# One gather per chosen expert for both expert tables, in eight shared buffers

## The chip, the core and the metric

The kernel runs on one core of a Trainium2 chip. The metric is the device time of one execution, in microseconds; lower is better. A core has five engines that each run their own list of instructions in order (TensorE, VectorE, ScalarE, GpSimd and SyncE; in the profile PE, DVE, ACT, POOL and SP) and sixteen DMA engines that move data between memory and the core's SBUF. The engines meet only through semaphores.

## The reference

One step of a two-layer trunk on 640 tokens (512 latent and 128 context tokens), all in float32. Each layer mixes tokens and then applies PEER, a lookup into 16384 experts. The change touches PEER alone:

```python
q = (xb @ wq).reshape(PEER_BLOCK, PEER_HEADS, 2, PEER_HALF)
s = jnp.einsum('thpd,hpnd->thpn', q, keys)
s_top, i_top = lax.top_k(s, PEER_TOPK)
cand = s_top[:, :, 0, :, None] + s_top[:, :, 1, None, :]
best, pos = lax.top_k(cand.reshape(..., PEER_TOPK * PEER_TOPK), PEER_TOPK)
g = jax.nn.softmax(best, axis=-1)
ue = jnp.take(u_tab, idx, axis=0)
ve = jnp.take(v_tab, idx, axis=0)
act = gelu(jnp.einsum('td,thkd->thk', xb, ue))
return jnp.einsum('thk,thkd->td', g * act, ve)
```

For each of 640 tokens and 8 heads, 16 experts are chosen. Each chosen expert has a row of 1024 numbers (4 KB) in table u, whose dot product with the token gives a weight, and a row of 1024 in table v, which is summed with that weight.

## The kernel before

The function `experts` does PEER for one layer; it runs twice. Its work is cut into 40 units: 8 heads (h) by 5 blocks of 128 tokens (b), a token on each partition. In a unit there are 16 choices s. For one unit n the steps are these.

- PE computes queries (`ask`, one call for two blocks, so three calls in five units, 48 matmuls each) and scores (`score`), three units ahead (LEAD).
- DVE turns scores into 16 row numbers per token (`choose(n + 2)`, some 25 short instructions that each wait for the one before), two units ahead. The row numbers are in `ex_index`.
- POOL issues indirect DMAs (`gather`): for each s one from `peer_u` into a slot of `u_row` and one from `peer_v` into a slot of `v_row`, each of 128 rows of 4 KB (0.5 MB). There are 8 slots for u (in `ring`) and 8 for v (in `early`). The v gathers run one unit behind the u gathers: POOL's list takes two u gathers of unit n and two v gathers of unit n - 1 in turn. A u slot is free when its dot product is made (`u_used`), a v slot when its matmuls are made (`v_used`).
- DVE makes 16 dot products, one per u slot, then waits for ACT's gelu on all 16, multiplies by the softmax share, and signals the 16 weights (`w_ready`). Then it runs `choose(n + 2)` and `gather_sum(n - 1)`, which adds the finished PSUM of a unit to the output.
- ACT makes one diagonal matrix for each choice (the identity times the column of weights), in 8 buffers.
- PE multiplies each diagonal with its v slot, and sums the 16 products of a unit in PSUM (`sums`, two matmul calls of 512 columns, four matmul records in the profile).

So DVE works on unit n while PE works on unit n - 1. The order on each engine is the order in which the code is written; nothing is scheduled otherwise. When the last unit's dots are done, PE still has its 16 choices to sum, and DVE uses this time for the layer norm of the earlier blocks (`residual`, `normal_rows`, `modulated`, `new_low_of`).

## Time and profile before

| | |
|---|---|
| Time, median of 3 runs | 6708.51 us (6702.12 to 6709.55) |
| The profiled execution, span | 7135.4 us |
| PE, DVE, ACT, POOL busy | 81%, 57%, 26%, 39% of the span |
| Gathers | 2560, 1342.34 MB |

The profiled execution is one execution with the profiler on. Its own time is its span, 7135.4 us, from the first instruction to the last; no other time of it is given. It is 427 us longer than the median of the unprofiled runs. Two stretches belong to `experts`: about 1648 to 3600 us and about 5182 to 7135 us.

The profile says for each engine how long it was busy, and for each instruction what ended the idle time before it. In a row of the timeline the number in square brackets is that idle time. A share of DMA near 1 means that all sixteen DMA engines had packets all the time. PEclk is TensorE's granted clock: 1.00 is 2.4 GHz and 0.50 is 1.2 GHz.

### The profile page before, as it was taken

The page shows a single profiled execution, that of the slowest core. Times are in us where ns is not written, and L with a number is a line of the kernel's source. Part 1 is how long each engine was busy: PE and PEld are TensorE (multiplying, and loading weights), DVE is VectorE, ACT ScalarE, POOL GpSimd, SP SyncE. Part 2 cuts the span into 40 slices and gives each one's busy share as a digit, 9 for nine tenths or more (in the row PEclk, how much of TensorE's full clock was granted, in tenths as well). Part 3 has the DMA queues.
Part 4 walks back from the last instruction along what each step waited for, and adds up shares of the span by engine and source line. Part 5 has one row for each costly group of instructions (what it writes and reads, how often), then busy time and mean ns, then how long its engine had stood idle before and what let it go on. Part 6 is the DMA issues. An engine that isn't in the chain of part 4 may idle for free. (4 is left out here: it accounts for less than half of the span.)

```text
span 7135.4 us, 94928 instructions
## 1 busy us (share of the span) xinstructions
PE 5756.5 (81%) x36912; PEld 4065.6 (57%) x36912; DVE 4044.6 (57%) x8218; ACT 1880.9 (26%) x3574; POOL 2797.2 (39%) x2909
## 2 busy tenths in 40 slices
PE   7889999795777777777788899997867777777776
PEld 7779999593333333333387799986833333333332
DVE  3654334557665666566636634346576566656666
ACT  1662112412222122212226621124121222122211
POOL 0330000014666666666613300000166666666665
PEclk8999999997998999999999999999988999999999
DMA  4002121327999999999921012222389999999998
GB/s 173 17 33 84 72 75 69 144 99 287 355 354 352 361 351 358 357 357 364 387 85 39 23 72 83 75 81 90 107 329 351 357 357 357 347 355 355 353 372 318
DMA packets 425299, 1632.88 MB, mean 229 GB/s; under 512 B 47648, under 2 KB 69600, under 8 KB 412260
## 3 DMA queue, kind: packets, MB, share of 16 engines
q0 software_dynamic: 368640, 1342.34, 49.4%
q1 hardware_dynamic: 56214, 284.46, 10.9%
q8 instruction: 297, 4.87, 0.3%
q14 instruction: 148, 1.21, 0.1%
HBM read 1611.68 MB, written 17.56 MB: 228 GB/s over the span
## 5 line engine op out<-in xcount | busy, mean ns | idle before, releaser
L1984 PE MATMUL ex_ps_y<-early,peer_small 128*128 128x512 f32 x5120 | 2534.4, 643 | 887.5 <-DMA early<-in_peer_v,ex_index 626.0
L1984 PEld LDWEIGHTS ex_ps_y<-early,peer_small 128*128 128x128 f32 x5120 | 993.4, 204 | 2348.5 <-issue 1416.5
L1834 DVE CUSTOM_DVE_ANT_0 ring<-ring,ex_ps_h 128x1024 f32<-128x1024 f32 x1280 | 1510.6, 1219 | 696.3 <-DMA ring<-in_peer_u,ex_index 545.1
L1637 POOL DMA_INDIRECT early<-in_peer_v,ex_index x1280 | 1234.7, 965 | 792.8 <-issue 355.8
L1637 POOL DMA_INDIRECT ring<-in_peer_u,ex_index x1280 | 1219.8, 953 | 706.5 <-issue 369.8
L1935 ACT ACTIVATE peer_small<-ident,ex_w 128x128 f32<-128x128 f32 x1280 | 441.2, 392 | 1477.2 <-PE ex_ps_y L1984 707.7
L1117 POOL TENSOR_SCALAR ring<-ring 128x2048 f32<-128x2048 f32 x2 | 10.8, 5387 | 1623.7 <-DMA ring<-mod_rows 1623.7
L258 PE MATMUL conv_ps<-h_high,conv_wh 128*128 128x320 f32 x1024 | 317.1, 310 | 9.3 <-DVE conv_wl L156 9.3
L258 PE MATMUL conv_ps<-h_low,conv_wh 128*128 128x320 f32 x1024 | 316.6, 309 | 0.0
L258 PE MATMUL conv_ps<-h_high,conv_wl 128*128 128x320 f32 x1024 | 316.5, 309 | 0.0
L1928 ACT ACTIVATE ex_act<-ex_dot 128x16 f32<-128x16 f32 x80 | 17.2, 216 | 1116.0 <-issue 944.7
L1965 PE MATMUL ex_ps_q<-h_high,ex_wh 128*128 128x256 f32 (+1 forms) x768 | 255.4, 333 | 57.7 <-DVE h_low L156 29.4
L258 PE MATMUL rf_ps<-rf_wh,h_high 128*128 128x256 f32 x960 | 268.2, 279 | 14.0 <-DVE rf_wl L156 14.0
L258 PE MATMUL rf_ps<-rf_wl,h_high 128*128 128x256 f32 x960 | 267.7, 279 | 0.0
L258 PE MATMUL rf_ps<-rf_wh,h_low 128*128 128x256 f32 x960 | 267.6, 279 | 0.0
L1965 PE MATMUL ex_ps_q<-h_low,ex_wh 128*128 128x256 f32 (+1 forms) x768 | 238.5, 311 | 26.5 <-issue 26.2
L1965 PE MATMUL ex_ps_q<-h_high,ex_wl 128*128 128x256 f32 (+1 forms) x768 | 239.7, 312 | 24.4 <-issue 24.1
L1038 POOL TENSOR_TENSOR room<-room,rec_bounds 128x256 f32<-128x256 f32 x80 | 64.7, 809 | 437.6 <-ACT room L1032 437.3
L1965 PEld LDWEIGHTS ex_ps_q<-h_high,ex_wh 128*128 128x128 f32 x768 | 171.0, 223 | 68.5 <-issue 37.9
L156 DVE TENSOR_TENSOR rf_wl<-ring,rf_wh 128x2048 fp32r<-128x2048 f32 (+1 forms) x36 | 74.7, 2085 | 238.5 <-ACT rf_wh L285 238.5
L156 DVE TENSOR_TENSOR conv_wl<-ring,conv_wh 128x2048 fp32r<-128x2048 f32 (+1 forms) x42 | 91.7, 2188 | 203.1 <-ACT conv_wh L285 203.1
L258 PEld LDWEIGHTS conv_ps<-h_high,conv_wh 128*128 128x128 f32 x1024 | 193.5, 189 | 9.8 <-DVE conv_wl L156 9.8
(335 smaller groups left out, 12091.3 us busy)
## 6 DMA issues: line engine op xcount, KB each, us to landing
ring<-in_w_in SPq DMA_DIRECT2D x54, 2048.0 KB, 7.8
ring<-in_mod_w SPq DMA_DIRECT2D x22, 2048.0 KB, 7.6
ring<-in_w_branch SPq DMA_DIRECT2D x12, 2048.0 KB, 7.8
ring<-in_peer_u,ex_index POOLq DMA_INDIRECT x1280
early<-in_peer_v,ex_index POOLq DMA_INDIRECT x1280
room<-in_peer_wq SPq DMA_DIRECT2D x14, 1024.0 KB
ring<-in_w_out SPq DMA_DIRECT2D x4, 2048.0 KB, 8.3
room<-mod_rows SPq DMA_DIRECT2D x12, 512.0 KB, 7.9
```

The costliest lines, as they stand in the source:

```text
L156: return nc.vector.tensor_tensor(low, full, high.bitcast(F32), ALU.subtract)
L258: last = nc.tensor.matmul(ps[:, at:at + cols], lhs, rhs, start=k == 0 and n == 0, stop=k == KT - 1 and n == 2)
L1038: step(nc.gpsimd.tensor_tensor(kk[:, m, at], kk[:, m, at], lb[:, 1, at], ALU.mult))
L1117: step(P_.tensor_scalar(vec[:, :, 1, :], vec[:, :, 1, :], 1.0, None, ALU.add))
L1637: nc.gpsimd.indirect_dma_start(rows[slot], None, table, bass.IndirectOffsetOnAxis(ap=index[n % 4][:, s:s + 1], axis=0)).then_inc(arrived[s ...
L1834: V.tensor_tensor_reduce(out=row, in0=row, in1=ps_h[:], scale=1.0, scalar=0.0, op0=ALU.mult, op1=ALU.add, accum_out=dot[n % 2][:, s:s + 1] ...
L1928: act.activation(act_v[n % 2][:], dot[n % 2][:], ACT.Gelu).then_inc(gelu_done, 1)
L1935: act.activation(diag[s % DIAGS], ident[:], ACT.Copy, scale=wgt[n % 2][:, s:s + 1]).then_inc(diag_ready, 1)
L1965: last = nc.tensor.matmul(ps_q[:, a, 0:width], w[h % 2][:, k, w_cols], h_split[x][:, k, toks], start=k == 0 and m == 0, stop=k == KT - 1 a ...
L1984: last = nc.tensor.matmul(ps_y[n % 2][:, c:c + 512], diag[s % DIAGS], v_row[s % V_SLOTS][:, c:c + 512], start=s == 0, stop=s == TOPK - 1)
```

## The change

The two tables are joined on the host into one, `peer_uv`, whose row is the u row and then the v row of an expert (8 KB). One gather fetches both into one of 8 slots; the slots lie in the same memory as the 16 of before. The slot is free when PE's matmuls on its v half are done. The v gathers are no longer a unit behind, so the dots and the sums of a unit run side by side: ACT makes gelu, weight and diagonal for each choice by itself, as soon as its dot is made. The softmax shares are made ahead (`soften`, `shares`). `ask` is split into two halves at s = 2 and s = 5, `score` is one choice later, and the work behind the last units' dots is arranged anew. `choose` is written in 16 parts, but all parts still run one after the other behind the unit's dots, with the same instructions.

```diff
-        U_SLOTS = V_SLOTS = DIAGS = 8
-        u_row, v_row = ([room[:]... for s in range(4)] for rooms in (ring, early))
+        SLOTS = DIAGS = 8
+        pair_row = [room[:]...[:, s * 2 * D:(s + 1) * 2 * D] for room in (*ring, *early) for s in range(2)]
+        u_row, v_row = ([row[:, side * D:(side + 1) * D] for row in pair_row] for side in range(2))
...
-                for n in range(units + 1):
-                    if n < units:
-                        pool.wait_ge(routed, n + 1)
-                    for s in range(0, TOPK, 2):
-                        if n < units:
-                            if TOPK * n + s >= U_SLOTS:
-                                pool.wait_ge(u_used, TOPK * n + s + 2 - U_SLOTS)
-                            for j in (s, s + 1):
-                                gather(u_row, u_in, T["peer_u"], n, j)
-                        if n:
-                            if TOPK * (n - 1) + s >= V_SLOTS:
-                                pool.wait_ge(v_used, TOPK * (n - 1) + s + 2 - V_SLOTS)
-                            for j in (s, s + 1):
-                                gather(v_row, v_in, T["peer_v"], n - 1, j)
+                for n in range(units):
+                    pool.wait_ge(routed, n + 1)
+                    for s in range(TOPK):
+                        if TOPK * n + s >= SLOTS:
+                            pool.wait_ge(v_used, TOPK * n + s + 1 - SLOTS)
+                        nc.gpsimd.indirect_dma_start(pair_row[s % SLOTS], None, T["peer_uv"], ...)
...
                         V.tensor_tensor_reduce(out=row, in0=row, in1=ps_h[:], ...
-                               op1=ALU.add, accum_out=dot[n % 2][:, s:s + 1]).then_inc(u_used, 1)
+                               op1=ALU.add, accum_out=dot[n % 2][:, s:s + 1]).then_inc(dotted, 1)
+                        if s == 7 and n + 1 < units:
+                            shares(n + 1)
                         behind_dot(n, s)
-                    dve.wait_ge(gelu_done, n + 1)
-                    V.reciprocal(total[n % 2][:], total[n % 2][:]).then_inc(recip_done, 1)
-                    V.scalar_tensor_tensor(wgt[n % 2][:], act_v[n % 2][:], total[n % 2][:], soft[n % 2][:], ...).then_inc(w_ready, 1)
-                    if n + 2 < units:
-                        choose(n + 2)
+                    for part in range(TOPK if n + 2 < units else 0):
+                        choose(n + 2, part)
...
-                    act.wait_ge(u_used, TOPK * (n + 1))
-                    act.activation(act_v[n % 2][:], dot[n % 2][:], ACT.Gelu).then_inc(gelu_done, 1)
-                    act.wait_ge(w_ready, n + 1)
                     for s in range(TOPK):
+                        act.wait_ge(dotted, r + 1)
+                        act.activation(act_v[n % 2][:, at], dot[n % 2][:, at], ACT.Gelu).then_inc(gelu_done, 1)
+                        act.wait_ge(gelu_done, r + 1)
+                        act.activation(wgt[n % 2][:, at], act_v[n % 2][:, at], ACT.Copy, scale=share[n % 2][:, at]).then_inc(weighed, 1)
+                        act.wait_ge(weighed, r + 1)
+                        act.activation(diag[s % DIAGS], ident[:], ACT.Copy, scale=wgt[n % 2][:, at]).then_inc(diag_ready, 1)
...
-                        if s == 2 and n and n + LEAD < units and where(n + LEAD)[1] % 2 == 0:
-                            ask(n + LEAD)
-                        if s == TOPK - 4 and n + LEAD < units:
+                        if s in (2, 5) and n and n + LEAD < units and where(n + LEAD)[1] % 2 == 0:
+                            ask(n + LEAD, (0,) if s == 2 else (1,))
+                        if s == TOPK - 3 and n + LEAD < units:
                             score(n + LEAD)
...
+        "peer_uv": np.concatenate([a["peer_u"], a["peer_v"]], axis=-1).reshape(DEPTH * EXPERTS, 2 * D),
```

What this does to the order is best seen on POOL and ACT. POOL, first layer, before: the end of unit 0's u gathers and the start of unit 1, where v gathers of unit 0 come in between (`ring_6` and `ring_7` hold u slots, `early_387` and `early_388` v slots, the number behind `ex_index` tells the unit).

```order
L1637 DMA ring_7<-in_peer_u,ex_index_394 128x1024 x4
L1637 DMA ring_6<-in_peer_u,ex_index_395 128x1024 x2
L1637 DMA early_387<-in_peer_v,ex_index_394 128x1024 x2
L1637 DMA ring_6<-in_peer_u,ex_index_395 128x1024 x2
L1637 DMA early_387<-in_peer_v,ex_index_394 128x1024 x2
L1637 DMA ring_7<-in_peer_u,ex_index_395 128x1024 x2
L1637 DMA early_388<-in_peer_v,ex_index_394 128x1024 x2
```

The same place in the changed kernel (the numbers behind the names are given anew in each build):

```order
L1643 DMA early_379<-in_peer_uv,ex_index_386 128x2048 x2
L1643 DMA early_380<-in_peer_uv,ex_index_386 128x2048 x2
L1643 DMA ring_6<-in_peer_uv,ex_index_387 128x2048 x2
L1643 DMA ring_7<-in_peer_uv,ex_index_387 128x2048 x2
L1643 DMA early_379<-in_peer_uv,ex_index_387 128x2048 x2
```

Half as many gathers, each twice as wide, and none of them a unit behind. ACT, one unit of the first layer before: the exponential, the gelu of all 16 choices, and 16 diagonals in a row.

```order
L1924 ACT_TABLE_LOAD
L1924 ACTIVATE ex_soft_406,ex_total_408<-ex_centred_400 128x16
L1928 ACT_TABLE_LOAD
L1928 ACTIVATE ex_act_404<-ex_dot_402 128x16
L1899 ACTIVATE ex_ps_h<-room_2 128x1024
L1935 ACTIVATE peer_small<-ident,ex_w_410 128x128 x7
```

The start of a unit in the changed kernel:

```order
L1944 ACT_TABLE_LOAD
L1944 ACTIVATE ex_soft_399,ex_total_401<-ex_centred_391 128x16
L1976 ACT_TABLE_LOAD
L1976 ACTIVATE ex_act_396<-ex_dot_394 128x1
L1980 ACTIVATE ex_w_404<-ex_act_396,ex_share_402 128x1
L1984 ACTIVATE peer_small<-ident,ex_w_404 128x128
L1976 ACTIVATE ex_act_396<-ex_dot_394 128x1
L1980 ACTIVATE ex_w_404<-ex_act_396,ex_share_402 128x1
L1984 ACTIVATE peer_small<-ident,ex_w_404 128x128
```

There are now three short instructions for each of the 16 choices, each behind the one before.

## Rows read from the trace of the kernel before

**Rows 1.** The page: span, busy time of each engine, gather queue (packets, MB, share).
```profile
span 7135.4 us, 94928 instructions
PE 5756.5 (81%) x36912; PEld 4065.6 (57%) x36912; DVE 4044.6 (57%) x8218; ACT 1880.9 (26%) x3574; POOL 2797.2 (39%) x2909
...
q0 software_dynamic: 368640, 1342.34, 49.4%
```
**Rows 2.** Stretches: length, busy time (count) of each engine, clock, DMA share, GB/s.
```profile
2500.00:3000.00 500.00, 381.02 (x1048) 182.79 (x1046) 318.07 (x767) 108.52 (x245) 320.06 (x335) 0.94 0.94 354
...
3500.00:3550.00 50.00, 35.20 (x69) 13.96 (x68) 36.64 (x51) 10.20 (x24) 31.51 (x31) 0.86 1.00 395
```
**Rows 3.** Gathers and matmuls by line, first layer: count, ns min/median/max, first to last start.
```profile
L1637 POOL DMA_INDIRECT ring<-in_peer_u,ex_index x640: 935/941/1992, 1648.0 to 3530.3; - x160
...
L1984 PE MATMUL ex_ps_y<-early,peer_small x2560: 589/592/1223, 1682.3 to 3578.9; 128*128 128x512 f32 x197
```
**Rows 4.** The same view, dot products, first layer.
```profile
L1834 DVE CUSTOM_DVE_ANT_0 ring<-ring,ex_ps_h x640: 1208/1218/1223, 1659.9 to 3543.6; 128x1024 f32<-128x1024 f32 x160
```
**Rows 5.** Timeline of POOL: start, us, engine, line, what, [idle before and what ended it].
```profile
2310.31 0.94 POOL L1637 DMA_INDIRECT ring<-in_peer_u,ex_index  x1 [0.30 <-issue]
2315.55 0.94 POOL L1637 DMA_INDIRECT early<-in_peer_v,ex_index  x1 [4.31 <-PE ex_ps_y L1984]
```
**Rows 6.** Timeline of PE: sums.
```profile
2313.31 3.70 PE L1984 MATMUL ex_ps_y<-early,peer_small 128*128 128x512 f32 x8 [1.40 <-DMA early<-in_peer_v,ex_index]
2319.75 4.12 PE L1984 MATMUL ex_ps_y<-early,peer_small 128*128 128x512 f32 x8 [2.74 <-DMA early<-in_peer_v,ex_index]
```
**Rows 7.** Stretches as in rows 2: PE nearly idle, right after it, and in full work.
```profile
2323.70:2327.20 3.50, 0.17 (x1) 0.00 (x0) 3.50 (x7) 0.40 (x1) 2.81 (x3) 1.00 0.98 382
2328.30:2331.60 3.30, 3.30 (x6) 1.24 (x5) 3.25 (x7) 0.40 (x1) 2.39 (x4) 0.50 1.02 401
2347.60:2351.30 3.70, 3.66 (x8) 1.44 (x8) 0.40 (x2) 2.03 (x5) 2.59 (x3) 1.00 1.02 409
```
**Rows 8.** Two calls of `ask` in the same view.
```profile
2355.90:2361.80 5.90, 5.90 (x51) 5.66 (x50) 4.84 (x26) 0.38 (x2) 4.57 (x5) 1.00 0.66 211
2261.40:2280.80 19.40, 7.89 (x51) 6.97 (x50) 13.80 (x24) 0.00 (x0) 11.87 (x13) 0.73 1.02 406
```
**Rows 9.** ACT groups, first layer: count | busy us, mean ns | idle before.
```profile
L1935 ACT ACTIVATE peer_small<-ident,ex_w 128x128 f32<-128x128 f32 x640 | 221.1, 393 | 752.0 <-PE ex_ps_y L1984 376.9 <-DMA scan_bmask<-in_bmask 222.4 <-issue 152.0
...
L1928 ACT ACTIVATE ex_act<-ex_dot 128x16 f32<-128x16 f32 x40 | 8.6, 216 | 558.1 <-issue 462.9 <-DVE ex_dot L1834 95.1
```
**Rows 10.** Timeline of DVE: one choice, its first instruction and what follows it.
```profile
2407.12 0.42 DVE L1674 COPY peer_small<-ex_ps_s 128x256 f32<-128x256 f32 x1 [8.28 <-remote]
...
2417.46 1.22 DVE L1742 TENSOR_TENSOR main<-main,ex_ps_y 128x1024 f32<-128x1024 f32 x1
```
**Rows 11.** DVE groups in the choices of the first layer, columns as in rows 9.
```profile
L1691 DVE MAX8 ex_best<-peer_small 128x8 f32<-128x256 f32 x40 | 17.1, 428 | 25.5 <-DVE peer_small L1688 16.0 <-remote 5.8 <-issue 1.0
L1696 DVE MAX8 ex_best<-peer_small 128x8 f32<-128x256 f32 x40 | 17.1, 428 | 10.7 <-remote 5.1
L1674 DVE COPY peer_small<-ex_ps_s 128x256 f32<-128x256 f32 x40 | 16.9, 423 | 153.8 <-remote 143.5 <-issue 7.9 <-PE ex_ps_s L1977 2.4
L1683 DVE MATCH_VALUE_LOAD ex_topi<-ex_top,peer_small 128x8 f32 x160 | 13.6, 85 | 21.1 <-issue 5.4 <-DVE ex_top L1679 5.3
L1687 DVE CAST ex_topf<-ex_topi 128x32 f32<-128x32 uint32 x40 | 7.6, 190 | 66.0 <-remote 55.9 <-issue 6.3 <-DVE ex_topi L1683 3.1
```
**Rows 12.** Timeline of DVE, end of the first layer.
```profile
3545.46 1.28 DVE L1774 SCALAR_TENSOR_TENSOR room<-room,norm_mv,room 128x1024 f32<-128x1024 f32 x1
...
3561.69 1.23 DVE L1781 TENSOR_TENSOR main<-main,ring 128x1024 f32<-128x1024 f32 x1
...
3579.82 1.21 DVE L1742 TENSOR_TENSOR main<-main,ex_ps_y 128x1024 f32<-128x1024 f32 x1
...
3599.34 1.22 DVE L156 TENSOR_TENSOR h_low<-ex_ps_h,h_high 128x1024 fp32r<-128x1024 f32 x1 [3.12 <-ACT h_high L1947]
```

More of the change, by code:

```diff
@@ L1547, in experts @@
         total = [sb(f"ex_total{j}", [P, 1]) for j in range(2)]
+        share = [sb(f"ex_share{j}", [P, TOPK]) for j in range(2)]
         wgt = [sb(f"ex_w{j}", [P, TOPK]) for j in range(2)]
@@ L1707, in choose @@
[L1707 to L1711 removed]
+                            last = V.max_index(top_i[:, a, 8:16], top[:, a, 8:16], lists[:, a, :])
@@ new lines, in choose @@
+                        chosen(4, last)
+                    if part == 5:
+                        behind(4)
+                        V.tensor_copy(top_f[:], top_i[:])
+                        chosen(5, V.tensor_tensor(cand[:].rearrange("p (i j) -> p i j", i=TOPK), top[:, 0, :].unsqueeze(2).to_broadcast([P, TOPK, TOPK]),
+                                                  top[:, 1, :].unsqueeze(1).to_broadcast([P, TOPK, TOPK]), ALU.add))
+                    if part == 6:
+                        behind(5)
+                        dve.sem_inc(picking, 1)
+                        chosen(6, V.max(best[:, 0:8], cand[:]))
@@ new lines, in choose @@
+                    if part == 13:
+                        behind(12)
+                        chosen(13, V.tensor_tensor(hit[:], hit[:], top_f[:].unsqueeze(2).to_broadcast(full), ALU.mult))
+                    if part == 14:
+                        behind(13)
+                        chosen(14, V.tensor_reduce(num[:], hit[:], AX.X, ALU.add))
+                    if part == 15:
+                        behind(14)
+                        chosen(15, V.scalar_tensor_tensor(num[:, 0], num[:, 0], float(P), num[:, 1], ALU.mult, ALU.add))
+                        behind(15)
+                        V.tensor_scalar(index[n % 4][:], num[:, 0], base[:, bass.ds(l, 1)], None, ALU.add).then_inc(routed, 1)
@@ L1823, in _ @@
                 dve.wait_ge(loaded, 48)
-                choose(0)
+                for part in range(TOPK):
+                    choose(0, part)
                 head_low_of(2)
                 head_low_of(3)
-                choose(1)
+                for part in range(TOPK):
+                    choose(1, part)
                 for n in range(units):
@@ L1854, in _ @@
                 normal_rows(2)
+                normal_rows(3)
                 if goes_on:
-                    dve.wait_ge(u_used, TOPK * units)
                     dve.wait_ge(vec_in, 64)
@@ L1860, in _ @@
                 onward(modulated, 1)
-                gather_sum(units - 2)
-                residual(3)
+                gather_sum(units - 1)
+                residual(4)
                 onward(new_low_of, 0)
                 onward(new_low_of, 1)
-                inverse(1, 3, 4)
-                normal_rows(3)
-                gather_sum(units - 1)
-                residual(4)
+                inverse(1, 4, 5)
+                normal_rows(4)
+                onward(modulated, 4)
                 onward(new_low_of, 2)
                 onward(new_low_of, 3)
-                inverse(2, 4, 5)
-                normal_rows(4)
-                onward(modulated, 4)
                 onward(new_low_of, 4)
@@ new lines, in _ @@
+                        act.wait_ge(weighed, r + 1)
+                        if r >= DIAGS:
+                            act.wait_ge(v_used, r + 1 - DIAGS)
+                        act.activation(diag[s % DIAGS], ident[:], ACT.Copy, scale=wgt[n % 2][:, at]).then_inc(diag_ready, 1)
+                        if s == 9 and n and n + LEAD < units and where(n + LEAD)[1] % 2 == 0:
+                            turn(n + LEAD)
+                        if s == 10 and b == 2 and h + 2 < PH:
+                            high(h + 2)
@@ L1942, in _ @@
+                        if s == 12 and n == units - 1:
+                            roots(4, 0, 4)
                 for b in range(NB):
                     if b == 2:
-                        roots(4, 3, 4)
+                        roots(5, 4, 5)
                     if goes_on:
@@ L1960, in ask @@
                         pe.wait_ge(turned, job)
-                    for a in range(2):
+                    for a in sides:
                         w_cols, toks = slice(a * P, (a + 1) * P), slice(b * P, b * P + width)
```

196 lines of the change are left out of this document (107 added, 89 removed).

## The prediction

> **What bounds the kernel now.** I read the page first, then the stretches, then the groups by line and last the timeline of single units. The page shows [rows 1] that no engine is full: PE 81% over the span, DVE 57%. The stretches show the reason: inside the expert work [rows 2] the DMA engines have packets 94% of the time over 500 us, at 354 GB/s, while PE is busy 76% and DVE 64%. So the gathers bound it, nearly. Their cost per unit comes out in two ways. The queue row [rows 1] gives the gathers 49.4% of sixteen engines' span, 0.494 x 7135.4 = 3525 us, over 80 units 44.1 us, over 16 choices 2.75 us for the 1 MB (u and v) of one choice. The full rate seen is 409 GB/s at share 1.02, in the last of [rows 7], which makes 1.049 MB / 409 = 2.56 us a choice and 41.0 us a unit. A layer's expert work, from the first gather at 1648.0 to the end of the last sum at 3579.5, takes 1931.5 us [rows 3], 48.3 us a unit. So some 4 us a unit are not transfer. They are bubbles such as the 4.31 us in which POOL waits for a v slot [rows 5], and single stalls of PE inside `ask` (19.4 us for work that takes 5.9 elsewhere [rows 8]).
>
> The profiled execution (its own time is its span) is 7135.4 us, 427 us over the median of 6708.5. The other stages move little data and their PE work is dense; I put all of the 427 us on the 80 units, 5.3 us each. An unprofiled unit of before is then 48.3 - 5.3 = 43.0 us, close to the 41.0 of pure transfer. That is an assumption, and much hangs on it: it leaves the old kernel only 2 us a unit to lose.
>
> **The change, part by part.** *Gathers.* The bytes stay the same. Half the packets and half the POOL instructions go (1280 x (0.94 + 0.30) = 1587 us of POOL time [rows 5]), but POOL was at 64% [rows 2] and no row shows the DMA waiting for it for long. What an 8 KB packet costs is not in the trace. From above: as much per byte as now, 2.75 us a choice; from below: the best rate of [rows 7], 2.56. I take 2.56 unprofiled, because the unprofiled unit of 43.0 leaves no room for 2.75 (16 x 2.75 = 44.0). What one `DMA_INDIRECT` of 8 KB rows costs POOL lies between 0.94 us (same number of rows) and twice that; I take 0.94.
>
> *Slots.* This is the part that decides. Before, u slots were free after a dot, and v slots filled behind them, so DMA had work while DVE chose. Now all 8 slots wait for one chain: dot, ACT, PE. While DVE runs the choice and `gather_sum`, no dot is made, and so no slot comes free; DMA has at most 8 choices of work, 8 x 2.56 = 20.5 us. I follow one unit from its first dot, with 8 slots full:
> - first dot 1.22 us [rows 4]; gelu 0.22, weight 0.22 (taken as the gelu), diagonal 0.39 [rows 9] and three hand-overs of some 0.1, together 1.1; the matmuls of a choice 1.85 us at full clock (8 records, two choices, in 3.70 [rows 6]). PE has been idle since the last sums, though: in [rows 7] a stretch with 0.17 us of PE work at clock 1.00 is followed by one at 0.50, that is 1.2 GHz. So 3.5 us for the first. Slot 0 is free after 5.8 us.
> - POOL issues; a gather into an idle queue was issued at 2315.55 [rows 5] and its matmul began at 2319.75 [rows 6], 4.2 us. 8 KB rows add half of 2.56: 5.5 us. Choice 8 is there at 11.3 us.
> - choices 9 to 15 follow at 2.56 each: 17.9 us, plus 0.6 as the second slot is freed at low clock too.
> - last dot 1.22, then the choice, then `gather_sum` 1.15 before the next dot.
> That makes 32.2 us plus the choice. The choice has the same 25 instructions. The undisturbed one takes 10.3 us, from 2407.12 to 2417.46 [rows 10]. Stalls inside it are in [rows 11]: 25.5 + 10.7 + 21.1 + 66.0 = 123 us over 40 units, 3.1 us each, of which about 0.7 is the ordinary hand-over: 2.4 us of stall, 12.7 us on average. Since the 5.3 us that the unprofiled unit lacks must come off something, I believe most of these stalls to belong to the profiled execution, and take 10.8. The unit is 43.0 us.
>
> *Queries.* `ask` costs 5.9 us when undisturbed [rows 8], in three of five units, and now stands in the chain that frees slots. Split in halves of some 2.9 us it delays the next slots by about what DMA can cover with the two slots already freed (5.1 us). From below nothing, from above the whole stall of [rows 8] in some units; I take 0.4 us a unit on average. Unit: 43.4 us.
>
> *Things that go.* The wait of DVE for the 16 gelus and the wait of the choice for its scores (153.8 us a layer before L1674 [rows 11]) go; both lay beside DMA that was working, so they pay nothing by themselves. The new gelus are 16 a unit, on an ACT at 22% [rows 2]: hidden, as 1.1 us a choice is less than PE's 1.85. The exponential with its two table loads comes while DVE chooses.
>
> *Ends.* The last unit's v half no longer follows a unit later. Before, 35 us lie between the last dot (3543.6 [rows 4]) and the last sum (3579.5 [rows 3]); now about 4. This is already in the sum below. But DVE used these 35 us for norm work, from 3545 on [rows 12]. Now two `normal_rows` (5.2 us), the vector (1.2), two `modulated` (4.9), the last residual and the low parts follow the last dot, some 33 us, where before 21 us followed the last sum (3579.5 to 3600.6 [rows 12]). From the last sum on that is 30 against 21, 9 us more in the first layer. In the second, without a next layer, it is 2.
>
> *Sum, unprofiled.* 38 units with a choice x 43.4 = 1649; two without, at the transfer rate, 2 x 41.0 = 82; 12 us from the first gather to the first dot [rows 3, 4]; 4 at the end: 1747 us a layer. Before: 1931.5 - 213.5 = 1718. So +29 a layer, twice, +58, and the ends +11: **+69, 6778 us**. Against the profiled execution's own time the same sum is: 2.75 a choice and 12.7 for the choice give 33.7 + 12.7 = 46.4, `ask` with its stalls 1.2, 47.6 a unit; 38 x 47.6 + 88 + 16 = 1913 against 1931.5, so -18 a layer, and a span near 7110. The profile should thus get a little shorter where the median gets a little longer.
>
> **Two rules of the Trainium skill.** Long stretches show 354 GB/s, but a short one 395 [rows 2] and a very short one 409 [rows 7]. The Trainium skill, "DMA: Bandwidth & Descriptors" (section "Where 436 GB/s comes from"), says that between HBM and SBUF the HBM side binds at about 358 GB/s for a core. By that a unit would be 16.8 MB / 358 = 46.9 us before and after, and nothing could be won or lost by the gathers. The short stretches speak against it. The same page ("Anatomy of one DMA — SWDGE (gpsimd) path") gives a gather about 2.0 us plus its bytes at 436 GB/s; an estimate by it is 4.4 us for 1 MB where I have 5.5, and the unit would be 1.1 us shorter.
>
> **Rivals.**
> 1. *The eight slots do cover the choice* (faster). If PE's clock does not fall in the gap, or has risen by the first sums, slot 0 is free after 4.2 us and the 0.6 goes: 4.2 + 5.5 + 17.9 + 2.4 + 10.3 = 40.3, less than the 41.0 of transfer, which then binds. 40 x 41.0 + 16 = 1656, -62 a layer, -113 in all with the ends: 6595. For it: my chain exceeds DMA's cover by under 2 us. Against it: [rows 7], where the clock falls after a far shorter gap.
> 2. *The stalls are there unprofiled* (slower). The choice takes 12.7 and `ask` adds 1.2: 46.1 us a unit, 38 x 46.1 + 82 + 16 = 1850, +132 a layer: 6984. It decides once the choice takes over 11 us. For it: stalls in every other unit in the trace. Against it: the 427 us.
> 3. *The wide gather does not do what it says*: POOL takes 1.9 us an issue, or a wide packet is slower. +0.95 us a unit in the chain: 6850. Nothing in the trace speaks for or against it.
>
> **How the numbers follow.** A change under 0.2% (6695 to 6722) can't be told from none. The forecast has 0.45, with its own range from 6690 to 6860 (choice of 10.3 to 11.8 us): 0.33 slower, 0.08 same, 0.04 faster. Rival 1 has 0.31 (0.30 faster, 0.01 same), rival 2 0.16, rival 3 0.08. Faster 0.34, same 0.09, slower 0.57. The range is 6580 to 6960: from just under rival 1 to just short of rival 2.
>
> **What would show it.** In the profile after: gathers at half the packets; one DMA gap of 1 to 5 us in each unit that has a choice, ended by POOL's issue after `ex_ps_y`; PEclk 0.50 at each unit's first sums; the dots of a unit as two groups, eight close together (1.14 us apart) and eight at the pace of arrivals; a unit of about 47.6 us. Wrong would be: DMA share at 0.98 or more in 500 us stretches (then rival 1), choices of over 12 us in most units with a slower median (rival 2), `DMA_INDIRECT` near 1.9 us (rival 3), or a ratio of span to median that stays as it is, which would fell the assumption on the 427 us.

## The result, and the profile after

The changed kernel takes 7003.56 us (median of 4 runs, 6991.94 to 7007.95), the kernel before 6705.32 in the same comparison: ratio 1.0442, 95% interval 1.0427 to 1.0456. In two later comparisons it took 7003.93 (ratio 1.044, 1.0419 to 1.046) and 7007.34 (1.0455, 1.0438 to 1.0473). The forecast was 6778, range 6580 to 6960: the direction was right, the size was not. One execution among all reported below, of the version with the choice in two runs, took 7123.35 us at a mean granted clock of 0.772 where its other three have 0.936 to 0.939; the ratios leave it out.

One fact first. The kernel before was profiled again (with the experiments below), and took 6693.5 us instead of 7135.4: the execution behind [rows 1 to 12] was a disturbed one. Its page, its stretch (columns as in [rows 2]) and its groups for three lines of the choice, first layer (columns as in [rows 9]):

```profile
span 6693.5 us, 94928 instructions
PE 5538.8 (83%) x36912; PEld 3956.3 (59%) x36912; DVE 4054.0 (61%) x8218; ACT 1887.1 (28%) x3574; POOL 2795.5 (42%) x2909
...
q0 software_dynamic: 368640, 1342.34, 50.6%
```
```profile
2500.00:3000.00 500.00, 397.43 (x1150) 185.88 (x1148) 356.80 (x853) 117.56 (x269) 364.57 (x382) 0.99 1.02 405
```
```profile
L1691 DVE MAX8 ex_best<-peer_small 128x8 f32<-128x256 f32 x40 | 17.1, 428 | 5.8
...
L1674 DVE COPY peer_small<-ex_ps_s 128x256 f32<-128x256 f32 x40 | 16.7, 417 | 1.9 <-PE ex_ps_s L1977 1.9
...
L1687 DVE CAST ex_topf<-ex_topi 128x32 f32<-128x32 uint32 x40 | 7.9, 197 | 1.4
```

So the old kernel has the DMA engines full (share 1.02, 405 GB/s, where [rows 2] have 0.94 and 354), and the stalls of [rows 11] are gone: 1.9 us a layer before L1674 instead of 153.8, 1.4 before L1687 instead of 66.0. The same view of the changed kernel, and its page with the groups that answer to [rows 1, 3]:

```profile
2500.00:3000.00 500.00, 389.81 (x1032) 186.52 (x1031) 321.44 (x778) 203.61 (x580) 166.92 (x176) 0.88 0.94 372
```
```profile
q0 software_dynamic: 184320, 1342.26, 48.4%
...
L2032 PE MATMUL ex_ps_y<-ring,peer_small 128*128 128x512 f32 x2560 | 1328.8, 673 | 473.0 <-ACT peer_small L1984 472.7
...
L1643 POOL DMA_INDIRECT ring<-in_peer_uv,ex_index x640 | 605.9, 947 | 1389.5 <-PE ex_ps_y L2032 1180.0
...
L1643 POOL DMA_INDIRECT early<-in_peer_uv,ex_index x640 | 623.3, 974 | 1152.8 <-PE ex_ps_y L2032 1097.4
...
L2025 PE MATMUL ex_ps_s<-room 128*128 128x128 f32 x320 | 78.2, 386 | 327.1 <-DVE peer_small L1672 325.7
```

Half the packets, the same bytes, and a DMA share that fell from 1.02 to 0.94. So the transfers no longer bind all the time. POOL's wait for matmuls on a slot, 2277 us (1180.0 + 1097.4), doesn't show this by itself: in the sixteen-piece version below it is still 1893 us, at a full DMA share. First and last gather and sum of the first layer, columns as in [rows 3], the undisturbed kernel before and then the changed one:

```profile
L1637 POOL DMA_INDIRECT ring<-in_peer_u,ex_index x640: 932/937/1792, 1643.6 to 3303.7; - x160
...
L1984 PE MATMUL ex_ps_y<-early,peer_small x2560: 589/593/1223, 1677.6 to 3359.0; 128*128 128x512 f32 x197
```
```profile
L1643 POOL DMA_INDIRECT ring<-in_peer_uv,ex_index x320: 932/937/2009, 1649.3 to 3463.8; - x160
...
L2032 PE MATMUL ex_ps_y<-early,peer_small x1280: 590/592/1190, 1677.8 to 3497.7; 128*128 128x512 f32 x183
```

From the first gather to the end of the last sum that is 1716.0 us before (3359.6 - 1643.6) and 1849.0 after (3498.3 - 1649.3): +133.0. The forecast had 1718 and 1747. The second layer adds +138.7, the stretches before, between and behind the two layers +24.8 (5.7, 13.4 and 5.7); together 296.5, which is 6990.0 - 6693.5. So the error lies in the 40 units of the changed kernel, 1849 against 1747, and a little in the ends. Now one unit without queries, in the timelines of DVE, POOL and PE:

```profile
2584.80 1.22 DVE L1876 CUSTOM_DVE_ANT_0 ring<-ring,ex_ps_h 128x1024 f32<-128x1024 f32 x1
...
2598.86 1.22 DVE L1876 CUSTOM_DVE_ANT_0 ring<-ring,ex_ps_h 128x1024 f32<-128x1024 f32 x1 [2.91 <-DMA ring<-in_peer_uv,ex_index]
...
2616.34 1.22 DVE L1876 CUSTOM_DVE_ANT_0 early<-early,ex_ps_h 128x1024 f32<-128x1024 f32 x1 [1.25 <-DMA early<-in_peer_uv,ex_index]
2617.48 0.42 DVE L1672 COPY peer_small<-ex_ps_s 128x256 f32<-128x256 f32 x1
...
2627.64 1.21 DVE L1778 TENSOR_TENSOR main<-main,ex_ps_y 128x1024 f32<-128x1024 f32 x1
2628.77 1.21 DVE L1876 CUSTOM_DVE_ANT_0 ring<-ring,ex_ps_h 128x1024 f32<-128x1024 f32 x1
```
```profile
2591.78 0.93 POOL L1643 DMA_INDIRECT ring<-in_peer_uv,ex_index  x1 [6.65 <-PE ex_ps_y L2032]
```
```profile
2587.22 9.26 PE L2032 MATMUL ex_ps_y<-ring,peer_small 128*128 128x512 f32 x16 [5.62 <-ACT peer_small L1984]
```
```profile
2587.20:2591.00 3.80, 3.78 (x5) 1.72 (x6) 3.80 (x7) 3.04 (x11) 0.00 (x0) 0.50 1.02 426
2591.00:2594.00 3.00, 3.00 (x7) 1.24 (x7) 1.96 (x4) 2.25 (x8) 1.07 (x2) 0.91 0.72 235
```

First dot at 2584.80, POOL's first gather 7.0 us later, the ninth choice's dot at 2598.86 (14.1), the sixteenth 17.5 later, then 12.4 us to the next unit's first dot, of which 10.2 are the choice (2617.48 to 2627.64). The unit is 44.0 us. The first sums ran at clock 0.50, and the DMA gap (share 0.72) follows them. The shape is the one forecast, eight dots close together and eight at the pace of arrivals. And one unit with queries:

```profile
2682.41 0.94 POOL L1643 DMA_INDIRECT ring<-in_peer_uv,ex_index  x1 [10.23 <-PE ex_ps_y L2032]
2685.25 0.94 POOL L1643 DMA_INDIRECT ring<-in_peer_uv,ex_index  x1 [1.90 <-PE ex_ps_y L2032]
2689.69 0.94 POOL L1643 DMA_INDIRECT ring<-in_peer_uv,ex_index  x1 [3.51 <-PE ex_ps_y L2032]
...
2697.58 0.94 POOL L1643 DMA_INDIRECT early<-in_peer_uv,ex_index  x1 [3.52 <-PE ex_ps_y L2032]
```
```profile
2675.43 1.21 DVE L1876 CUSTOM_DVE_ANT_0 ring<-ring,ex_ps_h 128x1024 f32<-128x1024 f32 x1
...
2687.97 1.22 DVE L1876 CUSTOM_DVE_ANT_0 ring<-ring,ex_ps_h 128x1024 f32<-128x1024 f32 x1 [2.98 <-DMA ring<-in_peer_uv,ex_index]
...
2710.32 1.22 DVE L1876 CUSTOM_DVE_ANT_0 early<-early,ex_ps_h 128x1024 f32<-128x1024 f32 x1 [1.25 <-DMA early<-in_peer_uv,ex_index]
...
2722.80 1.21 DVE L1876 CUSTOM_DVE_ANT_0 ring<-ring,ex_ps_h 128x1024 f32<-128x1024 f32 x1
```
```profile
2681.40:2684.10 2.70, 2.70 (x6) 1.19 (x4) 2.70 (x5) 2.15 (x9) 0.94 (x1) 0.57 0.19 46
...
2689.90:2691.90 2.00, 2.00 (x7) 0.94 (x5) 1.21 (x2) 0.29 (x1) 1.22 (x2) 1.00 0.46 78
```

The two halves of `ask` are the waits of 3.51 and 3.52 us. The ninth dot follows POOL's issue by 5.56 us (forecast 5.5), but from the ninth dot to the sixteenth it takes 22.35 us instead of 17.5, and the unit takes 47.4. The stretches show two gaps: the long one, DMA share 0.19, and a second, 0.46, made by the first half of the queries. Over five units, (2 x 44.0 + 3 x 47.4) / 5 = 46.0, and 1849.0 divided as in the forecast, (1849.0 - 82 - 16) / 38, is 46.1.

Two units are a small sample, so here are the means over units 2 to 36 of both layers, by the starts of the dots and gathers in this trace:

| from | to | 28 units without queries | 42 units with queries |
|---|---|---|---|
| first dot | POOL's gather into slot 0 | 6.9 | 6.9 |
| that gather | ninth dot | 5.8 | 5.6 |
| ninth dot | sixteenth dot | 19.0 | 22.3 |
| sixteenth dot | next unit's first dot | 12.5 | 12.5 |
| the whole unit | | 44.25 | 47.33 |

### The profile page after: what moved, and what is told of

Read it like the earlier page. It is cut to its first block and busy times, and to the rows that moved or that the text cites. A ratio compares the mean times of both kernels' runs of the same rounds, so it can differ in the third digit from the quotient of the medians.

```text
span 6990.0 us, 97627 instructions
## 1 busy us (share of the span) xinstructions
PE 5734.0 (82%) x36912; PEld 4086.5 (58%) x36912; DVE 4030.0 (58%) x8216; ACT 2580.7 (37%) x6050; POOL 1573.1 (23%) x1629
## 5 line engine op out<-in xcount | busy, mean ns | idle before, releaser
L2032 PE MATMUL ex_ps_y<-ring,peer_small 128*128 128x512 f32 x2560 | 1328.8, 673 | 473.0 <-ACT peer_small L1984 472.7
L2032 PE MATMUL ex_ps_y<-early,peer_small 128*128 128x512 f32 x2560 | 1266.4, 643 | 30.1 <-ACT peer_small L1984 29.9
L2032 PEld LDWEIGHTS ex_ps_y<-ring,peer_small 128*128 128x128 f32 x2560 | 542.3, 218 | 1210.1 <-issue 1209.9
L1876 DVE CUSTOM_DVE_ANT_0 ring<-ring,ex_ps_h 128x1024 f32<-128x1024 f32 x640 | 762.2, 1218 | 673.1 <-DMA ring<-in_peer_uv,ex_index 672.8
L1876 DVE CUSTOM_DVE_ANT_0 early<-early,ex_ps_h 128x1024 f32<-128x1024 f32 x640 | 764.7, 1218 | 481.0 <-DMA early<-in_peer_uv,ex_index 480.3
L1643 POOL DMA_INDIRECT ring<-in_peer_uv,ex_index x640 | 605.9, 947 | 1389.5 <-PE ex_ps_y L2032 1180.0
L2032 PEld LDWEIGHTS ex_ps_y<-early,peer_small 128*128 128x128 f32 x2560 | 521.7, 210 | 674.2 <-issue 673.8
L1643 POOL DMA_INDIRECT early<-in_peer_uv,ex_index x640 | 623.3, 974 | 1152.8 <-PE ex_ps_y L2032 1097.4
L1976 ACT ACTIVATE ex_act<-ex_dot 128x1 f32<-128x1 f32 x1280 | 258.2, 202 | 1610.2 <-DVE ex_dot L1876 1601.3
L1980 ACT ACTIVATE ex_w<-ex_act,ex_share 128x1 f32<-128x1 f32 x1280 | 376.9, 294 | 46.4
L2025 PE MATMUL ex_ps_s<-room 128*128 128x128 f32 x320 | 78.2, 386 | 327.1 <-DVE peer_small L1672 325.7
L2025 PEld LDWEIGHTS ex_ps_s<-room 128*128 128x128 f32 x320 | 59.9, 264 | 386.9 <-issue 385.2
```

The costliest lines, as they stand in the source:

```text
L1643: nc.gpsimd.indirect_dma_start(pair_row[s % SLOTS], None, T["peer_uv"], bass.IndirectOffsetOnAxis(ap=index[n % 4][:, s:s + 1], axis=0)).th ...
L1876: V.tensor_tensor_reduce(out=row, in0=row, in1=ps_h[:], scale=1.0, scalar=0.0, op0=ALU.mult, op1=ALU.add, accum_out=dot[n % 2][:, s:s + 1] ...
L1976: act.activation(act_v[n % 2][:, at], dot[n % 2][:, at], ACT.Gelu).then_inc(gelu_done, 1)
L1980: act.activation(wgt[n % 2][:, at], act_v[n % 2][:, at], ACT.Copy, scale=share[n % 2][:, at]).then_inc(weighed, 1)
L2025: last = nc.tensor.matmul(ps_s[:, a * P:(a + 1) * P], q_t[job % 2][:, a, toks], keys[:, 2 * h + a, :], start=True, stop=True)
L2032: last = nc.tensor.matmul(ps_y[n % 2][:, c:c + 512], diag[s % DIAGS], v_row[s % SLOTS][:, c:c + 512], start=s == 0, stop=s == TOPK - 1)
```

## The experiments

All times are medians. "The changed kernel" is 7003.6 us.

**The kernel before, profiled again** (no edit), twice.

> The kernel before, unchanged, profiled once more. Question: its profiled execution took 7135 us where its runs take 6705, while the profiled executions of the changed kernel and of the first experiments lie within 0.3% of their runs. If the extra 427 us belong to this kernel's own instructions under the profiler, the profiled span comes out again near 7100 (7050 to 7150) and the run near 6705. If the first profile caught a disturbed execution, the span comes out near 6705.

> The kernel before, profiled on the chip of this comparison. If its runs here take near 7110, the profile shows the stalls of the profiled execution of before (idle time ended by nothing on this core ahead of L1674 and L1687 of 100 us and more a layer); if they take near 6705, idle of 2 us there as in the second profile.

Measured 6695.26 us (span 6693.5) and 6716.13 (span 6714.3). The 427 us belonged to the one execution: profiling this kernel does not make them. Its 7135 us lie among the 7094 to 7147 that the kernel takes in one comparison below; no trace of those runs was kept, so whether the cause is the same is open.

**A part of the choice behind each dot.**

```diff
                         behind_dot(n, s)
-                    for part in range(TOPK if n + 2 < units else 0):
-                        choose(n + 2, part)
+                        if n + 2 < units:
+                            choose(n + 2, s)
```

> The changed kernel (7003.6 us) with part s of the choice behind dot s in place of all 16 parts behind the last dot. Theory A (all eight slots wait for dot, ACT and PE, and none comes free while DVE chooses; the profile after has an 11.2 us run between the last dot of a unit and the next first dot, and one DMA gap of some 3 us a unit behind it): the gap goes and the transfer binds, 16 x 2.64 = 42.3 us a unit in place of 46.1, 38 units twice, some -260 to -290 us: about 6730. Theory B (the halves of ask and the low PE clock alone make the gaps): the run goes but the gaps stay, 6850 to 6950. Theory C (the 8 KB gather is itself slower than two of 4 KB): no change, within 30 us of 7003.

Measured 6636.06 us, ratio 0.9886 (0.9867 to 0.9906), 367 us under the changed kernel. The stretch:

```profile
2500.00:3000.00 500.00, 415.36 (x1209) 192.72 (x1210) 354.50 (x873) 226.89 (x657) 184.51 (x194) 0.98 1.01 416
```

DMA share 1.01. With the choice cut up, the same gathers, slots and queries bring the transfers back to binding. The one long run is what costs. The expectation, some 6730, took 2.64 us a choice for the transfers; the kernel was faster than that.

**The choice in two runs of eight parts.**

```diff
-                    for part in range(TOPK if n + 2 < units else 0):
-                        choose(n + 2, part)
+                        for part in range(s - 7, s + 1) if s in (7, 15) and n + 2 < units else ():
+                            choose(n + 2, part)
```

> The choice of the next unit in two runs of eight parts, one behind dot 7 and one behind dot 15, instead of one run of sixteen parts behind dot 15. Theory A (a run of the choice costs only where it outlasts the slots already full; half a run is about 5.1 us, two slots' worth of transfer at 2.6 us): the transfers bind nearly all the time, 6640 to 6720, near the sixteen-piece version's 6636. Theory B (each stop of the dots costs its own restart of some 2 us, clock included): unit about 43.5 us, 6780 to 6850.

> The version with the choice in two runs of eight parts, beside the changed kernel. Where the kernel before takes near 6705: 6627, 5.4% below the changed kernel. Where it takes near 7110: theory A near 7050; theory B 6627.

Measured 6627.2 us (three runs of 6624.69 to 6628.51 and the one of 7123.35), ratio 0.9882 (0.9862 to 0.9902), and again, on one chip with the changed kernel (7007.34), 6627.01, ratio 0.9883 (0.9857 to 0.991). That is 1.2% under the kernel before. The sixteen pieces (6622.13 to 6644.02) and the two runs (6608.15 to 6642.56 the second time) are not to be told apart. The stretch:

```profile
2500.00:3000.00 500.00, 416.90 (x1205) 203.32 (x1206) 361.60 (x882) 225.42 (x651) 185.62 (x193) 0.93 1.01 416
```

The clock still falls to 0.93 on average and the queries are where they were, yet nothing is lost: a run of some 5 us fits under what the slots hold, one of 10 doesn't. The expectation of a cost for each stop is refuted.

**Four slots instead of eight.**

```diff
-        SLOTS = DIAGS = 8
+        SLOTS, DIAGS = 4, 8
```

> The changed kernel with four slots for gathered rows instead of eight (as many bytes, instructions and gathers). Theory A (while the choice runs no slot comes free, so each slot is worth one transfer of 2.6 us per unit): 4 x 2.6 = 10.4 us a unit more over 76 units, less up to 1 us a unit for queries that then lie beside arrivals: 7700 to 7800. Rival (the transfers keep their pace by slots that are freed during the unit, the loss is in the start and end of a layer): under 7200.

Measured 8132.88 us, ratio 1.2133 (1.211 to 1.2155): +1129, 14.9 us a unit where 10.4 were expected. The stretch, and POOL in the middle of a unit:

```profile
2500.00:3000.00 500.00, 335.90 (x831) 151.93 (x830) 254.66 (x605) 155.17 (x446) 127.85 (x133) 0.84 0.76 282
```
```profile
2574.34 0.93 POOL L1643 DMA_INDIRECT ring<-in_peer_uv,ex_index  x1 [7.91 <-PE ex_ps_y L2032]
...
2586.97 0.94 POOL L1643 DMA_INDIRECT ring<-in_peer_uv,ex_index  x1 [5.86 <-PE ex_ps_y L2032]
...
2601.08 0.94 POOL L1643 DMA_INDIRECT ring<-in_peer_uv,ex_index  x1 [6.80 <-PE ex_ps_y L2032]
```

Slots decide, and a slot was worth 3.7 us (14.9 / 4), over its 2.6 of transfer; the time lies above the expected range. POOL now waits more than once a unit: with four slots the way from gather to freed slot binds also between the choices.

**The queries behind the last sum.** (The scores and the copy of the queries move a unit with them.)

```diff
-                        if s in (2, 5) and n and n + LEAD < units and where(n + LEAD)[1] % 2 == 0:
-                            ask(n + LEAD, (0,) if s == 2 else (1,))
...
+                    if n and n + LEAD < units and where(n + LEAD)[1] % 2 == 0:
+                        ask(n + LEAD)
```

> The changed kernel with ask whole behind the last sum of a unit, while DVE chooses and PE has nothing to do, and its turn and score at s = 0 and s = 2 of the next unit. In the profile after, units with an ask take 47.1 us, those without 44.1. Theory A and B: 3.0 us in three of five units go, 24 units a layer, -140 us; and PE comes from work and not from rest to the first sums of these units, so the clock is up and up to 1.7 us more goes, -80: 6780 to 6870. Theory C: no change.

Measured 6863.38 us, ratio 1.0228 (1.0211 to 1.0245): 140 us under the changed kernel, 1.85 us a unit, where the forecast had 0.4 for all that the queries cost. The expected gain by the clock did not come: over units 3 to 35, POOL's gather into slot 0 starts 6.8 us after the first dot where the gap before had queries, and 7.0 where it had none. DMA share goes from 0.94 to 0.96:

```profile
2500.00:3000.00 500.00, 391.22 (x1092) 187.00 (x1093) 341.29 (x815) 212.49 (x613) 170.31 (x178) 0.91 0.96 386
```

**The queries in one piece at the third sum.**

```diff
-                        if s in (2, 5) and n and n + LEAD < units and where(n + LEAD)[1] % 2 == 0:
-                            ask(n + LEAD, (0,) if s == 2 else (1,))
+                        if s == 2 and n and n + LEAD < units and where(n + LEAD)[1] % 2 == 0:
+                            ask(n + LEAD)
```

> The changed kernel with the 48 matmuls of the queries in one piece ahead of the third sum, instead of halves ahead of the third and the sixth. The queries cost 3.0 us in a unit that has them, with the halves. Theory A (both halves stand in the chain that frees slots; a whole one delays slot 2 by 5.9 us instead of 2.9, and no later one): within 60 us of the changed kernel, 6940 to 7060. Rival (two slots ahead cover 5.1 us of it, as the prediction took it): 100 us faster or more, under 6900.

Measured 7023.07 us, ratio 1.048 (1.0459 to 1.0502), +20. Splitting them is worth almost nothing; where they stand is.

**Extra matmuls against the fallen clock.** Two placings of 128x128 matmuls whose results nobody reads: 14 behind the wait for the free accumulator and 10 ahead of the scores; then 16 ahead of that wait only.

```diff
+                    warm(16)
                     if n >= 2:
                         pe.wait_ge(y_out, n - 1)
```

> The changed kernel with 14 small matmuls of the identity (128x128 float32, result unused) ahead of a unit's first sum and 10 ahead of each score, where PE waits. Nothing else is changed. Theory A with the clock as a term: PEclk at the first sums is 1.00, the first slot is free 1.7 us earlier and the second up to 2.5 us, the DMA gap shrinks by that: -100 to -200 us, 6800 to 6900. If the clock does not matter: no change, or slower by what the small matmuls delay.

> The changed kernel with sixteen 128x128 matmuls (some 3.8 us at full clock, into a bank that nothing reads there) right behind a unit's last sum, in TensorE's idle gap ahead of the wait for the free accumulator, and none elsewhere. In the changed kernel the first eight sums take 8.5 us for sixteen matmuls at clock 0.5 where 7.0 would do. Theory A (the fallen clock is a part of the restart): the first sum is done 1.7 us earlier, 76 x 1 to 2.3 us: 6830 to 6930. If the clock still falls, or slot 0's transfer is hidden anyway: 6980 to 7020. If the extra matmuls outlast the gap: above 7020.

Measured 7067.91 us, ratio 1.0533 (1.0515 to 1.055), for the first, and 6924.06, ratio 1.0319 (1.03 to 1.0338), for the second. PE of the first, PE of the second, and the second's group of sums:

```profile
2705.44 5.28 PE L2037 MATMUL ex_ps_q<-ident 128*128 128x128 f32 x28 [5.14 <-DVE main L1778]
2710.56 3.60 PE L2032 MATMUL ex_ps_y<-ring,peer_small 128*128 128x512 f32 x8
```
```profile
2711.76 3.73 PE L2037 MATMUL ex_ps_q<-ident 128*128 128x128 f32 x32
2717.64 8.80 PE L2032 MATMUL ex_ps_y<-ring,peer_small 128*128 128x512 f32 x16 [2.14 <-ACT peer_small L1984]
```
```profile
L2032 PE MATMUL ex_ps_y<-ring,peer_small 128*128 128x512 f32 x2560 | 1218.8, 626 | 179.2 <-ACT peer_small L1984 179.0
```

In the first the sums ran at full clock (3.60 us for two choices), but behind 5.28 us of extra work: a dot and ACT are through 2.4 us after the same moment. Over units 3 to 35 of both layers the sums began 2.8 us late (5.26 us after the first dot instead of 2.42) for 1.8 us won on the first choice (1.88 instead of 3.68). In the second the idle time ahead of the sums on `ring` slots falls from 473.0 to 179.2 us and their mean from 673 to 626 ns, and the time by 80 us, 1.05 a unit. There the first choice takes 2.55 us on average and slot 0's gather starts 5.8 us after the first dot instead of 6.9. The fallen clock is a part of the restart, though in the unit shown the first sums are still slow.

**Both: queries behind the last sum, and 16 extra matmuls in the two of five gaps without queries.** (The two edits above, the second under a condition.)

> The changed kernel with two of the single edits together: the queries whole behind the last sum, and, in the two of five gaps that then have no queries, sixteen 128x128 matmuls into a bank that nothing reads there. Alone the first gave 140 us (1.85 us a unit), the second 80 us (1.05 a unit, over all five). Theory A (queries and fallen clock are two delays in one chain that frees the slots, and they add): 140 + 2/5 x 80 = 172 us less than the changed kernel, 6800 to 6850. Rival (whichever is removed first takes the gain, the other is hidden behind it, since the queries warm TensorE in the other gaps or not at all): no change from 6863. If the queries' own matmuls, ahead of the gap, also keep the clock up: 6780 to 6800.

> Queries behind the last sum and sixteen extra matmuls in the gaps without queries, beside the changed kernel on one chip. Theory A (the delays add): 172 us less than the changed kernel of this comparison, 6800 to 6850. Rival (one hides the other): 120 us less or fewer, 6880. It took 6882 on the other chip.

Measured 6882.48 us, but there the kernel before took 7118.98 (below), so it was run again beside the changed kernel (7003.93): 6863.99, ratio 1.0226 (1.0205 to 1.0246). That is the time of the queries alone (6863.38). The gains didn't add. The trace shows why the extra matmuls gave nothing; PE in one of the gaps that have them:

```profile
2714.69 3.73 PE L2037 MATMUL ex_ps_q<-ident 128*128 128x128 f32 x32
...
2724.44 6.71 PE L2032 MATMUL ex_ps_y<-ring,peer_small 128*128 128x512 f32 x8 [6.02 <-ACT peer_small L1984]
```

PE is idle for 6.0 us between the extra matmuls and the first sums, where it was some 2 us with the extra matmuls alone, and the first sums are slow again: 6.71 us for two choices, and 3.7 us for the first choice on average of these units. Moving the queries moved the scores too, and with them PE's wait ahead of them (327.1 / 80 = 4.1 us). With the queries moved alone, a gap that has none is 9.7 us long on average, where the changed kernel has 5.6, so matmuls placed at its start end too early. The same matmuls later in the gap were not tried.

**The scores behind the last sum.**

```diff
-                        if s == TOPK - 3 and n + LEAD < units:
-                            score(n + LEAD)
                         sums(n, s)
+                    if n + LEAD < units:
+                        score(n + LEAD)
```

> The changed kernel with the matmuls that compute the turn's scores placed behind the unit's last sum instead of between dots and sum. Rival R (the 327 us that TensorE waits on the row after the sixteenth dot, in the score, are on the path): 100 to 200 us shorter, 6800 to 6900. Theory A (the score only delays slots that the transfers don't need yet, since the DMA engines show no gap there): within 40 us of the changed kernel, 6960 to 7040.

Measured 7000.38 us, ratio 1.0439 (1.0422 to 1.0457): no change. The 327 us that PE waits at L2025 are new (the scores of the kernel before wait 2.7 us), and cost nothing.

**Two 4 KB gathers into the eight slots**, in the changed kernel and in the sixteen-piece version.

```diff
-                        nc.gpsimd.indirect_dma_start(pair_row[s % SLOTS], None, T["peer_uv"], ...
+                        nc.gpsimd.indirect_dma_start(u_row[s % SLOTS], None, T["peer_u"], ...
+                        nc.gpsimd.indirect_dma_start(v_row[s % SLOTS], None, T["peer_v"], ...
```

> The changed kernel with the two old tables: two gathers of 4 KB rows for each choice, into the same eight slots, u first. All else as in the changed kernel. Theory A: the same blocking; two POOL issues put 1.25 us more in front of the v rows but the u rows arrive 1.3 us earlier; 16 x (2.64 to 2.75) us of transfer: 7000 to 7090. Theory C: the transfer is as before, 6700 to 6800. On the 427 us by which the profiled execution of before is longer than its runs (the changed kernel's is not): if the number of packets or gathers makes them, the span here is 300 us or more over the run; if the v half a unit behind makes them, span and run agree within 30 us.

> The sixteen-piece version (a part of the choice behind each dot) with two 4 KB gathers a choice from the two old tables, into the same eight slots, instead of one 8 KB gather. There the DMA engines bind, so the packet's size shows undiluted. Theory A (a byte costs the same in 4 KB and 8 KB packets, within 1 to 3 per cent): 6600 to 6760. Rival (the wide packets are what made that version fast): above 6800. If two narrow gathers are again faster, as they were by 33 us in the one-run version, 6600 to 6636. The profiled span should tell whether the number of gathers makes the profiled execution longer than a run: near 7050 if so, within 0.5% of the run if not.

> The sixteen-piece version with two 4 KB gathers a choice. Where the kernel before takes near 6705: 6716, as before. Where it takes near 7110: near 7110 too if the 32 gathers a unit bring the stalls (theory B), near 6716 if it is the v gathers a unit behind or the choice in one run.

Measured 6970.63 us, ratio 1.039 (1.0373 to 1.0407), in the changed kernel, and in the sixteen-piece version 6715.76, ratio 1.0013 (1.0003 to 1.0022), and 6711.83, ratio 1.0006 (0.9994 to 1.0019). The stretch of the first, and the queue and stretch of the second:

```profile
2500.00:3000.00 500.00, 386.97 (x1045) 186.60 (x1044) 328.01 (x788) 208.26 (x596) 338.13 (x354) 0.89 0.98 375
```
```profile
q0 software_dynamic: 368640, 1342.34, 50.4%
```
```profile
2500.00:3000.00 500.00, 408.81 (x1146) 184.80 (x1144) 344.02 (x847) 220.04 (x640) 362.92 (x382) 0.97 1.02 406
```

Where the transfers bind, the wide gather saves 80 us, 0.06 us a choice (6715.8 - 6636.1, over 1280), and that is the whole gain of the good versions over the kernel before: with narrow gathers the sixteen-piece version takes within 0.2% as long as that kernel. In the changed kernel they don't bind, and the wide gather is 33 us worse than two narrow ones; the u half of a narrow pair lands sooner after the gap. Over units 2 to 36 the ninth dot follows POOL's issue by 4.5 us instead of 5.6 to 5.8, and the way from the ninth to the sixteenth takes 0.2 us longer with queries and 0.8 without.

**The changed kernel on other chips.**

> The changed kernel, unchanged. Where the kernel before takes near 6705: 7000, as before. Where it takes near 7110: theory A (the stalls strike whatever kernel has work in flight, as a property of the chip): 7150 to 7400. Theory B (they come with 32 gathers a unit on GpSimd, which the changed kernel has not): 7000, that is faster than the kernel before there.

> The changed kernel, unchanged. Where the kernel before takes near 6705: 7004. Where it takes near 7110: theory A (the stalls strike every kernel): 7150 to 7400; theory B (they come with 32 gathers a unit): near 7004.

Measured 7003.93 and 7007.34 us. In one of seven comparisons (that of the combined version) all seven runs of the kernel before took 7094 to 7147 us; neither of these two fell on such a chip. So theories A and B stay undecided, and whether the changed kernel would be the faster one there was not measured.

## Why the prediction was wrong

**The base** was right: 43.0 us an unprofiled unit forecast, 42.9 measured (1716.0 / 40). Taking 5.3 us off each unit of the profile was right in size: of the 441.9 us between the two profiled executions (7135.4 and 6693.5), 436.5 lie in the two layers (1931.5 - 1716.0 in the first, 1930.1 - 1709.2 in the second). But the forecast took them for what profiling adds, and they were the disturbance of one execution. It follows that the second half of the sum, the profiled one, was right by luck where it was right: the profile did get shorter while the median got longer, but to 6990.0 us with units of 46.1, not 7110 with 47.6. A profiled span 6% over the runs was a reason to doubt the rows, not only to subtract.

**The mechanism** was right: DVE's choice stops the dots, no slot comes free, and the DMA engines run dry in each unit, once without queries and twice with them. The one-run and two-run versions and the four slots show it. None of the signs that were listed for the rivals is there: no stretch at share 0.98 (rival 1), no gathers near 1.9 us on POOL (rival 3: means of 947 and 974 ns), no choice over 12 us (10.7 at most). The DMA gap, the clock of 0.50 at the first sums and the two groups of dots are there. Rival 2's 6984 is near the result for a wrong reason: it charged stalls of the choice, 12.7 us, where it takes 10.2.

**The steps that failed** are sizes in the chain of the unit, 46.1 us instead of 43.4:

| step | forecast | measured |
|---|---|---|
| `ask`, average a unit | 0.4 | 1.8 (3.1 x 22 / 38) |
| first dot to slot 0 free | 5.8 | 6.9 to POOL's issue |
| that issue to the ninth dot | 5.5 | 5.8 |
| seven more arrivals | 18.5 | 19.0 |
| last dot, choice, `gather_sum` | 13.2 | 12.5 |

(Measured are the means of the table above, without queries but for `ask`; 22 of the 38 units of a layer that have a choice have queries.)

`ask` is the largest: +1.4 us a unit, some 106 us of the 226 missed. It was set against "what DMA can cover with the two slots already freed (5.1 us)". But the queue had just run dry, so those two transfers were no reserve: the third gather came 4.4 us after the second (2685.25 to 2689.69) and the DMA share fell to 0.46. Taking the queries out gave 140 us back, splitting them only 20. The forecast named two bounds, nothing and "the whole stall of [rows 8] in some units", and took a value next to the lower one. Of the 5.9 us of work, 3.1 us were not covered in a unit with queries (47.33 - 44.25).

The restart (from the first dot until gathers flow again) is the second: +1.1 us up to POOL's issue. The first sum begins 2.4 us after the first dot and the first choice's sums take 3.7 us, near the 2.3 and 3.5 of the forecast. What the sum left out is the 0.81 us from the end of these sums to POOL's start, in each of the 70 units. The gather and the seven arrivals add 0.3 and 0.5. The choice was priced right in its undisturbed size, and the 0.5 us added for stalls was not there: -0.7. Together these four rows are +1.2.

The ends cost 24.8 us instead of 11. The sum then is 76 x (1.4 + 1.2) + 14 = 212 of the 226 us; most of the rest is in the first unit of each layer (48.1 and 48.9 us).

Rival 1 was given 0.31 because the chain exceeded the cover by under 2 us. The times in which two engines hand over to each other have no row of their own, and all that is left out makes such a chain longer.

## What to carry to other kernels

Before slots of two stages are joined, ask how long the engine that frees them is away in one piece, and count the slots' transfers against that run plus the restart; here eight slots hold 20 us, a run of 5 us is free and one of 10 costs 5 us a unit. Cut the run rather than move the rest: in this kernel two pieces brought 380 us, moving the queries 140, extra matmuls against the fallen clock 80, moving the visible wait of the scores nothing. And where a profiled execution is longer than the timed runs, take a second profile before any number is read from the first.

## What the hardware showed

- Sixteen DMA engines kept 416 GB/s over 500 us with 8 KB rows and 405 with 4 KB rows. The Trainium skill, "DMA: Bandwidth & Descriptors" (section "Where 436 GB/s comes from"), has the HBM side bind at about 358 GB/s for a core; its section "Measured (HBM→SBUF, 128 partitions, SWDGE, issued from GpSimd)" gives that figure for two cores that stream at once, and 425 GB/s for one alone. This kernel runs on one core, and its trace agrees with the latter: a unit's 16.8 MB take 40.3 us at 416 GB/s.
- In one comparison of seven all seven runs of the kernel before took 7094 to 7147 us, where the six others have 6693 to 6720. The combined version took 6882 there and 6864 elsewhere. What makes the old kernel sensitive was not settled.
- The profile adds nothing that shows: the profiled executions of the kernel before took 6695.26 and 6716.13 us, its other runs beside them 6699 to 6712 and 6693 to 6720.
- PE's clock was 0.50 at the first sums of a unit after a gap of 5.6 us (16 matmul records took 9.26 us; at full clock 7.03). Sixteen small matmuls took 47 ns off the mean of the sums on `ring` slots where they ended some 2 us ahead of the first sum, and nothing where they ended 6.0 us ahead.
- From the end of a choice's sums to the start of the gather that waited for them GpSimd needs 0.81 us by the profile (measured ahead of the first such gather of 70 units of the changed kernel).
